# A two-stack transformer on one core: gathering, weighing and scattering the token groups of the second stack's expert mixtures

## The reference, cut to what matters

```python
def hier_moe(h, wg, bg, we, be, w_gate, w_up, w_down):
    gl = (t @ wg + bg)                       # 256 x 4
    gp = softmax(gl);  _, gsel = top_k(gl, 1)
    g_oh = one_hot(gsel[:, 0], 4);  gw = sum(gp * g_oh)
    el = (t @ we + be).reshape(n, 4, 4)
    el_g = sum(el * g_oh[:, :, None], axis=1)
    tv, ti = top_k(el_g, 2);  tw = softmax(tv)
    w_grp = sum(one_hot(ti, 4) * tw[..., None], axis=1)
    comb = ((g_oh * gw)[:, :, None] * w_grp[:, None, :]).reshape(n, 16)
    a = silu(einsum('td,edf->tef', t, w_gate)) * einsum('td,edf->tef', t, w_up)
    return einsum('tef,efd->td', a * comb[:, :, None], w_down)
# x = x + g2 * hier_moe(h, ...), g2 a gate by feature
```

## Time and profile before

| | us |
|---|---|
| median of three runs | 2311.91 |
| lowest, highest | 2309.01, 2315.4 |
| span of the profiled execution | 2310.0 |
| mixture of layer 0 (gather begins to last add) | about 1800 to 1943 |
| mixture of layer 1 | about 2153 to 2297 |

### The profile page before, as it was taken

One profiled execution on the slowest core, in us unless ns is written; L12 is line 12 of the kernel. 1 busy time (PEld: TensorE's weight loads), 2 busy tenths in 40 slices (PEclk: granted clock), 3 DMA queues, 4 the chain that ended last, 5 costly groups with the idle time before them and its releaser, 6 DMA issues.

```text
span 2310.0 us, 32689 instructions
## 1 busy us (share of the span) xinstructions
PE 2220.6 (96%) x13834; PEld 1281.2 (55%) x13834; DVE 720.3 (31%) x1605; ACT 373.3 (16%) x805; POOL 1.2 (0%) x9
## 2 busy tenths in 40 slices
PE   7999999999989999999999999998998999989998
PEld 6867888888577333333333333333757435857433
DVE  4584312159776101101110101111342223163313
ACT  2102100010212111111110111111122212153311
POOL 0000000000000000000000000000000000000000
PEclk9999999999999999999999999998999999999999
DMA  9797254474266899999999999997600896910795
GB/s 330 246 368 261 94 219 161 166 266 164 101 236 255 329 395 388 408 404 408 404 408 405 409 404 409 401 409 283 255 1 6 323 409 246 253 46 1 277 409 212
DMA packets 232239, 644.98 MB, mean 279 GB/s; under 512 B 14715, under 2 KB 34449, under 8 KB 232081
## 3 DMA queue, kind: packets, MB, share of 16 engines
q1 hardware_dynamic: 229436, 638.16, 73.2%
q10 hardware_dynamic: 2645, 4.59, 0.6%
HBM read 641.67 MB, written 1.05 MB: 278 GB/s over the span
## 4 chain that ended last, share of the span: by engine, by line
PE 83%; DVE 9%; SPq 3%; DMA 2%; ACT 2%; issue 1%; ACTq 0%; DVEq 0%
PE bank L1765 19%; PE bank L1396 16%; PE bank L1914 10%; PE bank L1688 7%; PE bank L1810 4%; PE bank L1702 3%; DVE att L3403 3%; DVE att L3773 3%; SPq L1291 2%; PE bank L1864 2%; PE bank L1450 2%; DMA ring<-od_moe_down 2%; PE bank L1802 2%; PE bank L1974 1%; PE bank L1933 1%; PE bank L1411 1%
## 5 line engine op out<-in xcount | busy, mean ns | idle before, releaser
L1765 PE MATMUL bank<-ring,xn 128*32 128x512 f32 (+1 forms) x3424 | 443.3, 594 | 0.7 <-DMA ring<-od_moe_gu 0.7
L1396 PE MATMUL bank<-xn,ring 128*128 128x256 f32 x1664 | 371.6, 385 | 5.8 <-DMA ring<-ev_w_in 4.9
L1396 PEld LDWEIGHTS bank<-xn,ring 128*128 128x128 f32 x1664 | 320.7, 193 | 53.4 <-DMA ring<-ev_w_in 5.3
L1765 PEld LDWEIGHTS bank<-ring,xn 128*32 128x32 f32 (+1 forms) x3424 | 131.3, 115 | 287.1 <-issue 285.8
L1914 PE MATMUL bank<-ring,att 128*32 128x512 f32 x1824 | 201.0, 593 | 0.0
L3318 DVE TENSOR_TENSOR sq<-att,bank 32x512 f32<-32x512 f32 (+1 forms) x65 | 44.6, 686 | 392.0 <-ACT att L2673 390.6
L1688 PE MATMUL bank<-xn,ring 128*128 128x256 f32 x640 | 138.9, 379 | 0.0
L1914 PEld LDWEIGHTS bank<-ring,att 128*32 128x32 f32 x1824 | 58.4, 110 | 133.7 <-issue 133.3
L1688 PEld LDWEIGHTS bank<-xn,ring 128*128 128x128 f32 x640 | 121.6, 190 | 16.5
L2673 ACT ACTIVATE att<-bank 64x512 f32<-64x512 f32 (+1 forms) x115 | 67.9, 591 | 348.9 <-PE bank L1765 283.9
L2662 ACT COPY att<-bank 128x384 f32<-128x384 f32 (+1 forms) x72 | 29.1, 439 | 493.5 <-PE bank L1900 330.1
(11 more groups left out here) (415 smaller groups left out, 2182.7 us busy)
## 6 DMA issues: line engine op xcount, KB each, us to landing
ring<-od_moe_gu SPq DMA_DIRECT2D x196, 1024.0 KB, 17.3
ring<-od_moe_down SPq DMA_DIRECT2D x49, 2048.0 KB, 18.9
ring<-ada_w SPq DMA_DIRECT2D x24, 2048.0 KB, 8.1
ring<-moe_w_gate SPq DMA_DIRECT2D x32, 1024.0 KB, 16.6
ring<-moe_w_up SPq DMA_DIRECT2D x32, 1024.0 KB, 15.7
ring<-moe_w_down SPq DMA_DIRECT2D x16, 2048.0 KB, 20.1
z<-od_moe_gu SPq DMA_DIRECT2D x28, 1024.0 KB, 16.8
ring<-ev_w_in SPq DMA_DIRECT2D x10, 2048.0 KB, 20.0
```

Of the source, the lines that this page charges most:

```text
L1396: mm = nc.tensor.matmul(ps[:, c * T:(c + 1) * T], kblk(b)[:, k, u * T + c * P:u * T + (c + 1) * P], x[:, k, :], start=k == 0, stop=k == KD ...
L1765: mm = nc.tensor.matmul(PSB[r.fill.b][j * w:(j + 1) * w, :], xn[:, k, at:at + w], rows_[:, half, c * WBLK:(c + 1) * WBLK], start=k == 0, s ...
```

## The change

The gather takes 320 columns in place of 384: `g_take` now holds each group's slots once, side by side (96, 96, 64, 64). The slot weights are computed with the four weights on the partitions and the 320 slots along the row (2 matmuls), copied by DVE to `weight_rows`, and turned piece by piece by 14 small matmuls against the identity. The result of group 2 stays in partitions 0 to 63 of `y_slot`, that of group 3 goes to partitions 64 to 127, and one scatter with 128 rows serves both at the end. Cut to its core:

```diff
-        g_take = zf[:, EG * T:EG * T + EG * TC * PLACES].rearrange("p (g c n) -> p g c n", g=EG, c=TC)
+        g_take = zf[:, EG * T:EG * T + TC * GROUP_SLOTS].rearrange("p (c n) -> p c n", c=TC)
+        weight_rows = zf[0:EPG, at_z:at_z + GROUP_SLOTS]
@@ experts: order in which banks are dealt
+            r.row_fill = fill_turn((rows_weighed, count(rows_weighed, 1) + 1))
             r.weights_fill, r.weights = fill_turn((weights_ready, ...)), counted(weights_ready)
@@
-                if prev is not None:
+                if prev is not None and not prev.paired:
                     prev.h = counted(h_ready)
                     prev.out = four_fills(h_ready)
@@ PE
+            def scatter_groups(x, layer):
+                pe.wait_ge(*x.y[0].freed)
+                pe.wait_ge(y_beside, layer + 1)
+                pe.wait_ge(scatter_ready, x.scatter + 1)
+                for i, f in enumerate(x.out):
+                    ps = open_bank(f)
+                    scatter_pair(ps, i, P).then_inc(bank_full[f.b], 1)
@@ pe_experts
-                        mm = nc.tensor.matmul(ps[:, 0:EG * GROUP_CAP]..., xn_tok[...], g_take[:, :, c, 0:GROUP_CAP], ...)
+                        mm = nc.tensor.matmul(ps[:, 0:GROUP_SLOTS], xn_tok[...], g_take[:, c, :], ...)
                 pe.wait_ge(gather_ready, r.take + 2)
+                ps = open_bank(r.row_fill)
+                for c in range(TC):
+                    mm = nc.tensor.matmul(ps[0:EPG, 0:GROUP_SLOTS], comb_by[:, c, :], g_take[:, c, :], ...)
+                pe_spread(r.pos_fills, g_slot)
+                pe.wait_ge(rows_weighed, st.l + 1)
                 ps = open_bank(r.weights_fill)
-                        at = HP if GROUP_CAPS[g] == HP else i * HP
-                        for c in range(TC):
-                            mm = nc.tensor.matmul(..., g_take[:, g, c, at:at + P], comb_by[:, c, 2 * i:2 * i + 2], ...)
+                        for to, of, w in places:
+                            mm = nc.tensor.matmul(ps[to:to + w, 4 * g + 2 * i:4 * g + 2 * i + 2],
+                                                  weight_rows[:, GROUP_AT[g] + of:GROUP_AT[g] + of + w],
+                                                  ident[0:EPG, 2 * i:2 * i + 2], start=True, stop=True)
-                pe_spread(r.pos_fills, g_slot)
@@
-                    if prev is not None:
+                    if prev is not None and not prev.paired:
                         scatter_slots(prev, prev.scatter + 1)
@@
-                scatter_slots(prev, prev.scatter + 1)
+                scatter_groups(prev, st.l)
@@ ACT, copy_group_y
+                if x.beside:
+                    nc.scalar.copy(y_slot[HP:P, 0:512], full(x.y[0])[0:HP, :]).then_inc(y_ready, 1)
+                elif x.paired:
+                    nc.scalar.copy(y_slot[0:HP, 0:512], ps[0:HP, :])
+                    nc.scalar.copy(y_slot[0:HP, 512:D], ps[HP:P, :]).then_inc(y_ready, 1)
@@ DVE
-                takes(0, GROUP_CAP).then_inc(gather_ready, 1)
-                takes(GROUP_CAP, PLACES)
+                for c in range(TC):
+                    for g, w in ((0, GROUP_CAP), (2, HP)):
+                        ins = nc.vector.tensor_tensor(g_take[:, c, GROUP_AT[g]:GROUP_AT[g] + 2 * w]..., ALU.is_equal)
+                ins.then_inc(gather_ready, 1)
@@
+                nc.vector.tensor_copy(weight_rows, full(r.row_fill)[0:EPG, 0:GROUP_SLOTS]).then_inc(rows_weighed, 1)
@@
-                        add_group(prev)
+                        if not prev.paired:
+                            add_group(prev)
@@
+                nc.vector.tensor_copy(y_slot[HP:P, 512:D], full(prev.y[0])[HP:P, :]).then_inc(y_beside, 1)
                 add_group(prev)
```

55 lines of the change are left out of this document (30 added, 25 removed).

## The result

| us | before | after |
|---|---|---|
| median of the runs of this comparison | 2312.55 | 2300.87 |
| lowest, highest (4 runs each) | 2309.01, 2315.4 | 2297.84, 2301.71 |
| ratio with its 95% interval | | 0.9949 [0.9936, 0.9962] |
| span of the profiled execution | 2310.0 | 2300.1 |

The changed kernel is 0.51% faster; the forecast was 0.42% and 2302.2 us. The spans differ by 9.9 us, the sum of the forecast was 9.7.

A forecast was written before the change was run, and what follows sets the result against it. The prediction took PE to bound the mixtures, with the weight stream almost beside it. (1.5 + 3.65) + (0.9 + 3.65) = 9.7 us off the 2310.0 span gave 2300.3, plus 1.9 for the median 2302.2 us; range 2297 to 2308.5.

The forecast's parts named there:

- The order of bounds: In both mixtures PE bounds; the weight stream runs almost beside it, so PE's savings count only once weights have landed.
- Places: DVE ahead of the gather: four shorter place instructions instead of two, costing +0.1 us a mixture (bounds 0 and +0.2).
- Gather: 32 PE records of 320 columns instead of 384 save 1.75 us a mixture (bounds 1.5 and 2.0).
- Slot weights: Between gather and first product: -3.5 + 1.1 + 2.0 + 0.1 = -0.3 us a mixture (bounds -1.1 and +1.1).
- One scatter: Group 2's scatter goes from between group 3's last product and down products, saving 3.75 us; end scatter unchanged, 0.
- End copy: At each mixture's end ACT and DVE copy one half each, side by side: +0.1 us; +0.7 if they exclude one another.
- The cap by the stream: Up to group 3's last product PE's 1.95 us saving is limited by weight landings: 1.5 layer 0, 0.9 layer 1.
- the third, the clock: Rival, 15%: two more half-clock patches in each mixture give back 6.8 us; 2309.0 us, no change to be told.
- The fourth rival: Rival, 5%: waits for up weights at each mixture's first and last product bring long half clock; 2322 us, slower.
- The first rival: Rival, 13%: the stream isn't the wall, PE keeps 5.6 us a mixture; 2300.7 us, down to 2297.3.

The follow-up runs named there:

- slots alone: The changed kernel with two separate scatters and one ACT end copy as before, keeping the 320-column gather and new slot weights; 2310.96 us, 0.9991 of before.
- the repeat: The changed kernel, unedited, timed and traced once more; 2303.27 us, 0.996 of the kernel before.
- the copy uncovered: The changed kernel with the spread transposes put behind the small matmuls, so nothing covers DVE's copy of the rows; 2306.44 us, one time.
- without rows: The changed kernel with slot weights multiplied straight from `g_take` by 28 small matmuls, without `weight_rows` and DVE's copy; 2309.71 us, one time.
- half the up weights: The changed kernel loading only half of each up weight block in layer 1, which then computes with wrong weights; 2303.23 us, one time.
- one scatter alone: The kernel before with only the merged scatter and shared end copy, keeping its 384-column gather and old slot weights; 2306.86 us, 0.9972 of before.
- SP's reads late: The changed kernel with SP reading only the first group number ahead of the first weight loads; 2299.95 us, 0.9945 of before; again 2297.07 us, 0.9934.

## Why the prediction was right, step by step

- **The order of bounds** (PE bounds the mixture, the weight stream runs almost beside it). Shown, by four runs: slots alone gives its gain back as a wait, half the bytes take the wait away, an earlier stream shortens layer 0's mixture of the changed kernel by 0.9 us and those of the kernel before by nothing.
- **Places**, +0.1 taken. PE's idle time ahead of the gather is 2.15 us as before: 0.
- **Gather**, 1.75 taken. 12.25 to 10.54 us with a patch of half clock in it, 10.56 to 8.85 without (slots alone and the repeat): 1.71 both times.
- **Slot weights**, -0.3 taken. -3.47 + 1.17 + 1.70 + 0.09 for the spread = -0.5. The small matmuls took 1.70 and not 2.0, the wait that I had put at 0.1 did not occur; with the cover taken away it was 0.55.
- **One scatter**, 3.75, with 0 for the end. The middle is right: 3.75 us on the chain, 3.90 up to the end of the last down product, and turns and down products followed on. The 0 for the end is not: the forecast said that 128 rows instead of 64 stream the same 256 columns, but the scatter at the end took 3.69 us in place of 2.96, and 0.22 us of it reached the next stage.
- **End copy**, +0.1. The scatter starts 0.84 us behind the last down product instead of 0.76: +0.08; in turn it would have been +0.6.
- **The cap by the stream**, 1.95 allowed down to 1.5 in layer 0 and 0.9 in layer 1. From the gather to the start of the last scatter, the end copy included, it is -5.11 and -5.08 us. For layer 0 that is the forecast (1.5 + 3.65 = 5.15), with the wait of 0.7 us at the place that was named. For layer 1 it was mis-sized, 0.9 + 3.65 = 4.55 forecast: the forecast asked whether the patch of half clock in the first product stays or goes, and gave 0.9 as a middle. In this trace it went, and one stood in the gather in its place. A slow gather leaves the stream time to get ahead, so there was no wait at the first product, and the whole of 1.5 came out. The first up weights helped: they landed 12.7 us behind SP's first issue (2152.2 + 10.6 against 2150.08), before it was 13.9.

Up to the next stage's first matmul the two mixtures are 4.89 and 4.85 us shorter, 9.74 in all. Outside them layer 0's gather starts 1.2 us later, and the parts between and behind the mixtures are 1.4 us shorter together, which makes the 9.9. The mechanism was right; that the sum came out at 9.7 is in part luck, since layer 1's gain, 0.5 us above its middle value, made up for the 0.2 us of the end scatter in each mixture, and the parts outside nearly cancelled.

Of the rivals the third, the clock, came nearest to being a second truth. In the first trace of the changed kernel the number of patches did not grow. In its repeat the gathers had none, but PE waited 1.15 and 1.82 us at the first products with half clock behind, and the mixtures took 134.31 and 133.84 us instead of 132.8: 2.6 us for both. Its two medians, 2300.87 and 2303.27, are 2.4 apart, but with a trace of one execution each that may be chance. That is less than the 6.8 us of the rival, since there a patch in the first product stands in the place of that in the gather and not beside it. Beside it stand the two in layer 0 of the run with the copy uncovered and of that without rows, so the rival's case exists, but in none of the timed runs of the changed kernel did it reach its 2309.0.

The fourth rival has the right mechanism, wait and then half clock, and the wrong size: 1.3 to 2.9 us of half clock and 0.8 to 2.4 of waiting at one place in a mixture. It needed 2.4 us at each of two places to undo the gain, and was priced at 5. The forecast's argument against it, that its waits were 1.6 us and less, was itself too low. The first rival is refuted for this kernel: without the wall PE would have kept 0.7 to 1.0 us more in each mixture, as the run with half the up weights showed.

Open: what decides in a given execution whether the gather has the patch. The same program had it in both gathers in one trace and in neither in another, with the same fillers, idle time and handover ahead of it. What starts the patches in and behind the small matmuls is open too: they stand in the first product of layer 1 before the change, in the two-column matmuls of layer 1 with one scatter alone, and not behind the same small matmuls with SP's reads late; no run varies the small matmuls or the length of the wait by itself. Nor is it settled why the spread was slow in the run with the copy uncovered, and why the first product of layer 0 was slow in the run without rows.

## What to carry to other kernels

Before you count what a faster engine saves, list for each load when it lands and when its first reader starts; the smallest slack is the gain that you are sure of, and the rest comes back as a wait, here more at the first load than at the last. Savings behind the last load of a stage count in full, so make those first. And a stream that never pauses ends earlier only by fewer bytes or an earlier start: look at what its queue does ahead of the first transfer, here three register reads of 0.55 us that were on no critical path until PE had become faster.

## What the runs showed of the hardware

- Two-column matmuls are paid mainly by the columns that are loaded, whether 4 or 128 rows stand behind them: some 0.83 ns a column by the weight loads of 32, 64 and 96 columns (103, 132, 156 ns with 4 rows; 110, 137, 164 with 128). 28 records with 1536 columns took 1.70 us, 56 with 3072 took 2.75, 32 with 4096 took 3.47.
- 56 records in 2.75 us are 49 ns each. The Trainium skill ("TensorE: Matmul & The Clock Gate", "Wait — 56ns, not 53.3ns?") gives 62 ns for a small matmul where the sequencer decodes; the 28 records meet it (61 ns each), the 56 stay below it, so here it is no floor for a record.
- 16 records of 256 columns took 2.96 us with 64 rows and 3.69 us with 128, both at a granted clock of 1.00 and both at the end of a mixture. Why is not shown.
- Copies of half a bank cost what copies of the whole one do (0.58 us on ACT, 0.69 on DVE for 64 rows as for 128), and on two engines they run side by side.
- PE's clock was near 1.2 GHz for part of the next 3.4 to 3.6 us (granted 0.50 to 0.67) behind all nine waits of 1.1 to 2.4 us for a DMA. It stayed up behind those of 0.16 to 0.82 us, but for one of 0.80 us, ahead of which it had already fallen. Behind an idle time of 2.15 us ahead of the gather it fell in some executions and not in others, and behind one of 0.21 us in none of four. It also fell in or behind series of two-column matmuls with no wait since the gather (granted 0.58 over 3.50 us in the earlier trace rows).
- The weight stream has a fixed pace: 116.3 to 116.4 us from the first issue of a mixture to the landing of its last up weights, in both layers of the kernels before and after, at 402 to 416 GB/s in the windows behind the waits, as before.
- A read of one number into SP's registers costs 0.27 us and 0.15 more for its arithmetic, some 0.55 with the gaps, and all of them stand ahead of the loads in SP's queue.
